# Two boundaries with a norm taken in halves of 256 tokens, beside the products on either side

## The reference

```python
mix = jnp.einsum('bsd,de->bse', merged, w_out)
x = x + rmsnorm(mix, norm_mix_post)

h = rmsnorm(x, norm_ffn_pre)
gu = jnp.einsum('bsd,df->bsf', h, w_ffn_up)
gate, up = jnp.split(gu, 2, axis=-1)
ff = jnp.einsum('bsf,fd->bsd', jax.nn.silu(gate) * up, w_ffn_down)
x = x + rmsnorm(ff, norm_ffn_post)
...
h = rms_norm(x, norm_g)            # the second layer
proj = jnp.einsum('bsd,de->bse', h, w_in)
```

## Time and profile before

| what | us |
|---|---|
| runs of the kernel (3): median | 1049.77 |
| lowest and highest | 1049.70, 1050.35 |
| span of the profiled execution | 1048.5 |
| TensorE busy in it | 1027.9 (98%) |
| VectorE, ScalarE, GpSimd busy in it | 522.6, 458.7, 517.6 |

### The profile page before, as it was taken

The page is one execution under the profiler, slowest core; times in us unless marked ns, Lnnn a source line. Parts: engine busy times, 40 slices in busy tenths (PEclk is TensorE's granted clock), DMA queues, the critical chain, the costliest instruction groups (busy, mean ns, idle before and its releaser), DMA issues.

```text
span 1048.5 us, 13344 instructions
## 1 busy us (share of the span) xinstructions
PE 1027.9 (98%) x4914; PEld 846.5 (81%) x4914; DVE 522.6 (50%) x839; ACT 458.7 (44%) x667; POOL 517.6 (49%) x300
## 2 busy tenths in 40 slices
PE   7999999999999999999999999999999999999998
PEld 5888888788888787888888888887888887777787
DVE  6899785554361555434334311003624176685731
ACT  5322345888752433323333232223354357476540
POOL 3444565933534423444444446445285554665562
PEclk9999999999999999999999999999999999999999
DMA  7232221111142313322323233334122211111112
GB/s 232 98 101 95 87 83 58 61 61 61 61 181 86 115 41 101 99 87 94 100 100 100 93 108 101 100 100 141 41 80 81 81 61 42 61 55 47 41 61 81
DMA packets 25965, 91.03 MB, mean 87 GB/s; under 512 B 3008, under 2 KB 3136, under 8 KB 25792
## 3 DMA queue, kind: packets, MB, share of 16 engines
q1 hardware_dynamic: 25920, 90.42, 25.9%
HBM read 88.31 MB, written 2.10 MB: 86 GB/s over the span
## 4 chain that ended last, share of the span: by engine, by line
PE 87%; DVE 4%; POOL 3%; issue 3%; ACT 1%; DMA 1%; SPq 0%; POOLq 0%; DVEq 0%; ACTq 0%
PE ps L443 26%; PE ps L445 26%; PE ps L444 26%; POOL w_lo L2187 2%; PE ps L841 1%; PE ps L865 1%; DVE s L2028 1%; PE ps L589 1%; POOL sp_lo L2239 1%; PE ps L583 1%; PE ps L485 1%; PE ps L569 1%; DMA w_raw<-weights 1%; PE ps L472 0%; DVE pt_lo L1564 0%
## 5 line engine op out<-in xcount | busy, mean ns | idle before, releaser
L2187 POOL TENSOR_TENSOR w_lo<-w_raw,w_hi 128x1024 fp32r<-128x1024 f32 x146 | 347.7, 2382 | 426.0 <-ACT w_hi L1042 376.8
L1042 ACT ACTIVATE w_hi<-w_raw 128x1024 fp32r<-128x1024 f32 (+1 forms) x140 | 146.3, 1045 | 289.4 <-PE ps L445 289.4
L443 PE MATMUL ps<-a_hi,w_hi 128*128 128x512 f32 x560 | 224.1, 400 | 10.3 <-DVE w_lo L1564 7.1
L445 PE MATMUL ps<-a_hi,w_lo 128*128 128x512 f32 x560 | 218.9, 391 | 0.0
L444 PE MATMUL ps<-a_lo,w_hi 128*128 128x512 f32 x560 | 218.8, 391 | 0.0
L443 PE MATMUL ps<-b_hi,w_hi 128*128 128x512 f32 x408 | 159.4, 391 | 1.1 <-POOL w_lo L2187 0.8
L445 PE MATMUL ps<-b_hi,w_lo 128*128 128x512 f32 x408 | 158.8, 389 | 0.0
L444 PE MATMUL ps<-b_lo,w_hi 128*128 128x512 f32 x408 | 158.7, 389 | 0.0
L443 PEld LDWEIGHTS ps<-a_hi,w_hi 128*128 128x128 f32 x560 | 105.5, 188 | 37.1 <-issue 9.1
L445 PEld LDWEIGHTS ps<-a_hi,w_lo 128*128 128x128 f32 x560 | 105.6, 188 | 22.7
L444 PEld LDWEIGHTS ps<-a_lo,w_hi 128*128 128x128 f32 x560 | 105.7, 189 | 21.0 <-issue 0.5
(11 more groups left out here) (326 smaller groups left out, 1600.8 us busy)
## 6 DMA issues: line engine op xcount, KB each, us to landing
w_raw<-weights SPq DMA_DIRECT2D x159, 512.0 KB, 3.2
resid<-x_t SPq DMA_DIRECT2D x8, 256.0 KB, 5.8
resid<-x_t SPq DMA_DIRECT2D x1, 2048.0 KB, 8.2
out_t<-out_sb SPq DMA_DIRECT2D x8, 256.0 KB, 2.0
w_raw<-weights SPq DMA_DIRECT2D x2, 256.0 KB, 4.7
vec<-vecs SPq DMA_DIRECT2D x1, 220.0 KB, 9.1
vec<-vecs SPq DMA_DIRECT2D x1, 4.0 KB, 1.8
```

Of the source, the lines that this page charges most:

```text
L443: pe.matmul(out, s_hi, m_hi, start=first, stop=False, skip_group_check=True)
L445: return pe.matmul(out, s_lo, m_hi, start=False, stop=last, skip_group_check=True)
L1042: act.activation(w_hi[:, k % 2, 0:width], w_raw[:, k, 0:width], ACT.Copy).then_inc(hi_ready, 1)
L2187: pool.tensor_tensor(w_lo[:, k % 2, 0:width], w_raw[:, k, 0:width], w_hi[:, k % 2, 0:width].bitcast(F32), ALU.subtract).then_inc(lo_ready, 1)
```

## The change

Both boundaries are taken in two halves of 256 tokens (`HALVES`). The last two tiles of w_out, and the last of w_down, are computed for the first half of the tokens, then for the second (`half_unit`, matmuls of 256 columns, each half in a bank of its own). The norm of the first half runs while TensorE is at the second half of these tiles, and the residual of the first half is followed by the first four units of the next stage for that half; the norm of the second half comes in between, after chunk 4. `extra` is gone. `wx` now holds all four first units of the up projection, and a new slot `wz` holds one unit at each boundary; both loops over tiles are written out. `norm` takes a range of token blocks, so that VectorE's operations in a boundary are 128 x 256, two for each one of before, in `new_residual`; the squares of the new residual and their additions stay 512 wide.

The diff, cut to its core. TensorE:

```diff
-            def extra(count, src):
-                for _ in range(count):
-                    pe.matmul(ps[:, 5, :], tri[:, :], src, start=True, stop=True, skip_group_check=True)
+            def half_unit(bank, half, s_hi, s_lo, m_hi, m_lo, chunks, at_chunk=0, first=0, last=KC - 1):
+                tok = HALVES[half]
+                for c in chunks:
+                    w = slice(c * P, (c + 1) * P)
+                    mm = products(ps[:, bank, tok], s_hi[:, w], s_lo[:, w], m_hi[:, at_chunk + c, tok], m_lo[:, at_chunk + c, tok],
+                                  first=at_chunk + c == first, last=at_chunk + c == last)
+                return mm
...
+                for c in range(KC):
+                    if c == 4:
+                        second_spread()
+                    pe.wait_ge(first_lo, n_first + c + 1)
+                    pieces(0, (2, 3) if c < 2 else (2, 3, 0) if c < 4 else range(4), (c,))
+                    if c == 0:
+                        last_total()
+                    if c == 1:
+                        pieces(0, (0,), (0, 1))
+                    if c == 3:
+                        pieces(0, (1,), range(4))
                 for c in range(KC):
                     pe.wait_ge(split_lo, fresh + c + 1)
+                    pieces(1, range(4) if c < 2 else (0, 1), (c,))
+                pieces(1, (2,), range(2, KC))
+                pieces(1, (3,), range(2, KC))
...
-            with pe.Fori(0, 2) as i:
-                four_tiles(i, U_WO, T_WO, a_hi, a_lo, fresh=KC + CC)
-            pe.wait_ge(acc_ready, 2)
-            total_part(sq_m, 0, True, False)
-            extra(4, a_hi[:, 0, :])
-            pe.wait_ge(sq_ready, 2 * KC + CC)
-            total_part(sq_m, KC - 1, False, True)
-            extra(6, a_hi[:, 0, :])
-            spread(r_exp2, 1)
-            extra(15, a_hi[:, 0, :])
-            first_four(U_UP, T_UP, b_hi, b_lo, wx_hi, wx_lo, 2 * KC + CC)
+            half_unit(2, 0, *w6, a_hi, a_lo, range(KC)).then_inc(first_done, 1)
+            half_unit(3, 0, *w7, a_hi, a_lo, range(KC)).then_inc(first_done, 1)
+            half_unit(0, 1, *w6, a_hi, a_lo, range(4))
+            first_total(sq_m, first_acc, 1, 2)
+            half_unit(0, 1, *w6, a_hi, a_lo, range(4, KC)).then_inc(units_done, 1)
+            half_unit(1, 1, *w7, a_hi, a_lo, range(4))
+            spread(r_exp2, 1, (0, 1))
+            pe.wait_ge(acc_ready, 2)
+            total_part(sq_m, 0, True, False, (2, 3))
+            half_unit(1, 1, *w7, a_hi, a_lo, range(4, KC)).then_inc(units_done, 1)
...
```

ScalarE and VectorE:

```diff
-            split_next(U_UP, 0)
-            split_next(U_UP, 1)
+            def next_up(c):
+                if c in (3, 6):
+                    split_first(U_UP + 4, c // 3 - 1, w_hi[:, c // 3 - 1, :])
...
+                for c in range(KC):
+                    high(1, c)
                     act.activation(sq[:, c, :], resid[:, c, :], ACT.Square).then_inc(sq_ready, 1)
+                    second(c)
...
+            for k in (0, 1):
+                act.wait_ge(units_done, U_Q2 + 2 - k)
+                split_first(U_Q2 + 4, k, w_hi[:, k, :])
...
+                norm(q, D, r_exp, 0, 2)
+                after_norm()
                 dve.wait_ge(row_ready, q + 1)
                 for c in range(KC):
+                    residual(0, c)
                     if c:
+                        lows(0, c - 1)
+                    if c == 2:
+                        after_second()
+                    if c == 4:
+                        norm(q + 1, D, r_exp, 2, 4)
+                lows(0, KC - 1)
+                dve.wait_ge(row_ready, q + 2)
+                for c in range(KC):
+                    residual(1, c)
+                    if c:
+                        lows(1, c - 1)
+                lows(1, KC - 1)
                 for c in range(1, KC):
                     add_square(sq, n_sq, c)
```

More of the change, by code:

```diff
@@ L467, in four_tiles, with total_part @@
                               late=late if k == 0 else None)
-            def total_part(sq, c, first, last):
-                for b in range(TB):
+            def total_part(sq, c, first, last, blocks=range(TB)):
+                for b in blocks:
                     mm = pe.matmul(ps[:, 6, b:b + 1], sq[:, c, b * P:(b + 1) * P], ones[:, 0:1],
-                                   start=first and b == 0, stop=last, skip_group_check=True)
+                                   start=first and b == blocks[0], stop=last, skip_group_check=True)
                 if last:
@@ L720, in _ @@
             pe.wait_ge(split_lo, 3 * KC + CC + 16)
[L721 to L737, removed]
+            for t in range(KC - 1):
+                pe.wait_ge(tile_drained, T_DN + t + 1)
+                for r in range(DN_UNITS):
+                    if t == 0 and r == 2:
+                        pe.wait_ge(split_lo, 3 * KC + CC + FC)
+                    m = DN_UNITS * t + r
+                    unit_tile(U_DN + m, m % 2, t % 4, h_hi, h_lo, chunks=DN_CHUNKS[r],
+                              at_chunk=8 * r, first=r == 0, last=r == DN_UNITS - 1)
@@ new lines, in _, with last_down @@
+            down = (((w_hi[:, 1, :], w_lo[:, 1, :]), 0, 8), ((wz_hi[:, :], wz_lo[:, :]), 16, 6), ((w_hi[:, 0, :], w_lo[:, 0, :]), 8, 8))
+            def last_down(bank, half, part, cs=None):
+                w, at_chunk, count = down[part]
+                return half_unit(bank, half, *w, h_hi, h_lo, range(count) if cs is None else cs, at_chunk, 0, -1)
+            pe.wait_ge(tile_drained, T_DN + 8)
+            for part in range(DN_UNITS):
+                pe.wait_ge(lo_ready, U_DN + 21 + part + 1)
+                mm = last_down(3, 0, part)
@@ L1275, in _, with half_square @@
             act.preload_act_table(ACT.Sqrt)
-            for j in range(KC):
+            def half_square(sq, j, bank, half, done, n, ready):
+                act.wait_ge(done, n)
+                act.activation(sq[:, j, HALVES[half]], ps[:, bank, HALVES[half]], ACT.Square).then_inc(ready, 1)
+            for j in range(KC - 2):
                 act.wait_ge(units_done, U_WO + j + 1)
                 act.activation(sq_m[:, j, :], ps[:, j % 4, :], ACT.Square).then_inc(sq_ready, 1)
-                if j < 6:
+                if j < 5:
@@ L1322, in _ @@
             act.preload_act_table(ACT.Sqrt)
-            for j in range(KC):
+            for j in range(KC - 1):
                 for r in range(DN_UNITS):
@@ L1579, in newton, with norm @@
                 V.wait()
-            def norm(q, count, r_exp):
-                var, t, r = (ps[:, 6, n * TB:(n + 1) * TB] for n in (1, 2, 3))
-                y = ncol[:, 1, :]
+            def norm(q, count, r_exp, first=0, last=TB):
+                var, t, r = (ps[:, 6, n * TB + first:n * TB + last] for n in (1, 2, 3))
+                y = ncol[:, 1, first:last]
                 dve.wait_ge(stat_ready, q + 1)
-                ts(var, ps[:, 6, 0:TB], 1.0 / count, ALU.mult, EPS, ALU.add).then_inc(var_ready, 1)
+                ts(var, ps[:, 6, first:last], 1.0 / count, ALU.mult, EPS, ALU.add).then_inc(var_ready, 1)
                 dve.wait_ge(std_ready, q + 1)
-                V.do(dve.reciprocal(y, ncol[:, 0, :]))
+                V.do(dve.reciprocal(y, ncol[:, 0, first:last]))
                 V.wait()
@@ L1605, in add_square @@
                 V.wait()
-                add = V.do if c < last else (lambda x: x.then_inc(acc_ready, 1))
+                add = V.do if c != last else (lambda x: x.then_inc(acc_ready, 1))
                 add(tt(sq[:, 0, :], sq[:, 0, :], sq[:, c, :], ALU.add))
@@ L1861, in _, with copy_tiles, half_copy @@
             att_low(KC - 1)
-            def copy_tiles(dst, sq, n_sq):
-                for j in range(KC):
+            def copy_tiles(dst, sq, n_sq, count, added):
+                for j in range(count):
                     dve.wait_ge(sq_ready, n_sq + j + 1)
                     if 0 < j < KC - 1:
-                        add_square(sq, n_sq, j, last=KC - 2)
+                        add_square(sq, n_sq, j, last=added)
                     dve.tensor_copy(dst[:, j, :], ps[:, j % 4, :]).then_inc(tile_drained, 1)
-            def new_residual(q, src, sq, n_sq, gain_post, gain_next, dst_hi, dst_lo, n_hi, r_exp):
-                norm(q, D, r_exp)
+            def half_copy(dst, j, bank, half):
+                dve.tensor_copy(dst[:, j, HALVES[half]], ps[:, bank, HALVES[half]]).then_inc(tile_drained if half else first_drained, 1)
@@ L1898, in up_pairs @@
+            new_residual(1, mix, sq_m, 2 * KC + CC, "g_mix_post", "g_ffn_pre", b_hi, b_lo, 0, 2 * KC + CC, r_exp2, (7, 0), mix_sixth, mix_last)
             def up_pairs(i, banks):
```

240 lines of the change are left out of this document (166 added, 74 removed).

## The result

The changed kernel takes 1058.99 us (median, 1056.95 to 1059.23) against 1049.77 before (1049.44 to 1050.35): ratio 1.0079, 95% interval 1.0067 to 1.0090. By the medians it is slower by 9.2 us, where 4.1 was forecast, and lies outside the forecast range of 1047.6 to 1057.0. The profiled span is 1057.3, 8.8 above that of before.

The account below looks back on a forecast made before the run. TensorE, busy 98%, was taken to bound the kernel, with VectorE ending both boundaries last after the change. Sums 2.8 and 1.3 us later, 4.1 together, on 1049.77 gave 1053.9 us; range 1047.6 to 1057.0.

Parts of the forecast that it names:

- The price of halves: Both boundaries: 256-column products 0.12 us, VectorE chunks 1.25; sums at 40.3 and 42.9 us, together 4.8 gained without crossings.
- the one at tile 6: First boundary: the fourth unit's GpSimd low part holds VectorE's half addition of tile 6, 0.5 us on the start.
- GpSimd against VectorE: Both boundaries: GpSimd low parts hold VectorE operations with two SBUF inputs; sums 2.8 and 1.3 us later than before.
- (a): Rival for both boundaries: crossings cost little, the gain of 4.8 us stays, 1045.0; 18%.
- (b): Rival for both boundaries: half of the crossings bite, two at 2.3 us against the 4.8, 1049.6; 20%.
- The clock: TensorE behind its boundary stalls: the main forecast counted no slow products, leaving a clock fall to a rival.
- rival (c): Second boundary: TensorE's clock falls in the 4.5 us wait, eight slow products cost 1.7 us, 1055.6; 18%.
- Rival (d): 256-wide products bound by weight load, 0.19 us apart; the 612 would cost 43 us more; 2%.

Follow-up runs that it names:

- no_crossing: Changed kernel with GpSimd's low parts of the fifth and sixth unit behind each boundary signalled but not made: 1046.04 us, ratio 0.9965.
- fill: Changed kernel with idling products where TensorE stood still, 8, 1, 2 and 9 at the first boundary, 20 at the second: 1055.06 us, ratio 1.0052.
- full_feed_early_row: full_feed with the sum after ten of the fifth unit's 16 high products and the transposes between fifth and sixth unit: 1043.64 us, ratio 0.9932.
- full_feed: high_first with GpSimd's low parts held behind VectorE's additions, the first boundary's splits moved, and TensorE's units and products reordered: 1050.57 us, ratio 1.0007.
- high_first: Changed kernel with the fifth unit's 16 high products before the sum and the transposes in the middle of the sixth unit: 1060.98 us, ratio 1.0112.
- late_low: Changed kernel with GpSimd's low part of the fifth unit held back at both boundaries until VectorE's additions have ended: 1052.36 us, ratio 1.0023.

## Why the prediction was wrong, point by point

- **The price of halves** held. Products of 256 columns came 0.12 apart, the chunk took 1.25 us, its operations 0.48 and 0.42, the additions 5.45. In no_crossing the sums stood at 40.31 and 42.84. The forecast had 40.3 and 42.9 without any crossing; no_crossing still has the one at tile 6, priced at 0.5, so the first came 0.5 earlier than the terms say. From the zeros to the sums that is 1.65 and 3.16 us, 4.8 together, less than before (41.96 and 46.0); in the time of the whole kernel 3.9 are seen (1046.04).
- **GpSimd against VectorE** held, with its places and sizes: two low parts of over 2 us, two additions the same (4.6 us over all seven), the half addition of tile 6 at 1.35. Sums with the clock up (fill): 44.27 and 47.49, forecast 44.7 and 47.3. The Trainium skill ("SBUF — State Buffer", section "Who interferes with whom") says that a VectorE instruction with two SBUF inputs contends with a GpSimd one that reads SBUF. The trace agrees, at 256 columns too, which no row of before showed: 2.55 and 2.29 us instead of 0.48. Rivals (a), cheap crossings, and (b), half of them, are out: with the clock up (fill against no_crossing) the four operations move the sums by 3.96 and 4.65 us, where the terms had 4.0 and 4.4.
- **The clock is the step that failed.** The sum put the clock's cost at nothing. It had TensorE stall about 2.5 us in each of two waits at the first boundary and 4.5 at the second, and asked after the clock only for the 4.5, as rival (c), for 1.7 us and 18%. The clock fell at both. At the first it fell behind stalls of 2.01 and 0.27 us, and the slow products made TensorE end 1.1 us after VectorE (+0.94 on the sum). At the second it slowed the sum (1.72 for 0.81) and ten products: 2.95. The 1.7 of rival (c) came from eight products at the start and left the sum out. fill, which changes nothing but TensorE's idleness, gives back 3.9 of the 5.1 us by which the forecast was short. The Trainium skill ("TensorE: Matmul & The Clock Gate", section "HAM oscillation — how this bites in real kernels") has idle gaps bring the lower clock back, and the trace agrees for the 4.62 us at the second boundary. The gaps of that section are longer than 2.01 us; that this was enough at the first boundary is shown by this trace alone.
- **The remaining 1.2 us** (1055.06 against 1053.9). In fill's trace the sums are off by -0.4 and +0.2, and +0.6 lie between the boundaries, 0.4 of them the longer wait for w_lo that the forecast did not have; +0.2 lie behind the second sum. The rest, about 0.6, is not settled: the start of the first boundary varies from 339.47 (fill) to 341.47 (full_feed_early_row) over kernels that are alike up to there, which is more than what is missing.
- **Rival (d)** is out: the products of 256 columns came 0.12 apart, not 0.19.

That the removed idling products did work for the clock is shown from both sides: their removal from the kernel before costs 1.9 us although the boundaries themselves get shorter, and adding others after the change gives 3.9 back.

## What to carry to other kernels

When a stage is cut finer, look at which operations of a second engine now fall among those of the engine that sets its end: here four GpSimd subtractions of 2.4 us, which had lain behind VectorE's chain, turned a gain of 3.9 us into a loss of 9.2, clock included. Every wait that a forecast puts on TensorE is to be priced twice, for itself and for the slow products that may follow it, and where it can't be removed, work that needs nothing late (high products ahead of the low ones, a sum moved behind them) or idling products belong into it. And when a step is moved to a later place on the engine that feeds, read what is queued behind the one that waits for it: full_feed lost 6.9 us to a sum placed six products later and transposes placed half a unit later.

## What the runs showed of the hardware

- The length of a wait of TensorE alone doesn't decide whether its clock falls. It fell behind waits of 1.03 us (high_first, second boundary), 1.37 (late_low, first boundary: 13 products at 0.43 us), 1.82 (high_first), 2.01 (after), 2.73 (full_feed) and 4.62 (after); it did not behind 1.31 (high_first, full_feed), 1.37 (late_low, second boundary) and 1.83 (full_feed). What decides it was not tried.
- GpSimd's memset of 128x1024 beside VectorE's operations with two SBUF inputs cost them nothing, its subtraction of the same size made them up to 2.1 us longer.
- Executions of the same instructions differ by up to 2.0 us at the start of the first boundary (fill and full_feed_early_row), and this arises in the first 16 us. Windows of fill and of late_low, whose first boundaries start 1.76 us apart (in the first bracket, the products that run in the window, counted also where they only reach into it):

```profile
10.00:12.00 2.00, 1.70 (x7) 1.02 (x7) 2.00 (x4) 2.00 (x4) 0.00 (x0) 1.00 1.04 395
12.00:14.00 2.00, 2.00 (x11) 1.57 (x10) 1.70 (x3) 1.43 (x4) 0.00 (x0) 1.00 1.03 420
```
```profile
10.00:12.00 2.00, 1.88 (x4) 1.06 (x5) 1.78 (x3) 1.99 (x4) 0.00 (x0) 1.00 1.01 376
12.00:14.00 2.00, 2.00 (x5) 1.54 (x6) 2.00 (x4) 1.56 (x3) 0.00 (x0) 1.00 1.04 424
```

By the timelines TensorE starts 15 products in these 4 us in fill and 7 in late_low, where they come 0.43 apart for longer; eight products of 0.227 are the 1.8 us. The column of the granted clock reads 1.00 in both, so at the start of an execution the distance between products says more than that column.
